# Seven products of halves instead of eight for 46 more weight chunks of a three-block transformer kernel

## The chip, the cores and the metric

One core of a Trainium2 chip runs the whole program. The metric is the device time of one execution in microseconds (us). PE is TensorE, DVE is VectorE, ACT is ScalarE, POOL is GpSimd, SP is SyncE, whose queue issues the weight transfers.

## What is computed

The reference takes 512 tokens of width 1024 through two layers of a first block and one of a second, all in 32-bit floats. What matters here are its large products of tokens and weights:

```python
# first block, twice
proj = x @ w_in[l]                       # 1024 x 8192: q, k, v, conv (3 x 512), memory query, gates (3 x 1024)
merged = (g[:, :, 0] * (y_attn @ w_br_attn[l]) + g[:, :, 1] * (y_conv @ w_br_conv[l])
          + g[:, :, 2] * (y_mem @ w_br_mem[l]))
mix = merged @ w_out[l]                  # then layer norm, 16 routed experts, layer norm
# second block, once
proj = h @ w_in                          # recurrent branch, state-space (S5) branch, gates (2 x 1024)
mixed = (g_rwkv * o_rwkv + g_s5 * o_s5) @ w_out[l]
z = h @ w_up                             # then convolution, gelu(gate) * val, @ w_down
```

Queries and keys are then rotated by position, the attention's output is normalised by head, and the gates go through a sigmoid.

## The kernel before, in words

**Tiles and chunks.** Tokens lie transposed: a buffer (XT, B[0] to B[5]) holds 8 tiles of 128 features x 512 tokens. Weights come in chunks of 2 MB, 1024 rows by 512 columns, into a ring of four slots. A chunk gives four output tiles. `project` (L445 to L452) makes one tile: 8 contraction steps (4 for br_conv, br_mem, br_rwkv and br_s5) of a 128x128 weight block against 512 tokens, into one of eight PSUM banks. A 32-bit matmul is two instructions in the trace, so a tile of 8 steps shows 16 of them, at L451.

**The ring.** The order of the chunks is a list (`layer_chunks`, L123; `SECOND`, L148). `place_stream` (L171) deals them to the slots in turn. SP issues them in this order (`issue_weights`, L327), each when the last user of its slot has ended, and waits in order. Some entries of the list are "unfilled": they take a slot as work space and nothing is loaded.

**Stages.** The program is a row of stages; at each stage's end all engines meet. The stages that the change touches: `qkv` (L465: 6 chunks; queries and keys are copied by ACT, rotated by a matmul at L491 and turned by DVE), `conv_and_memory_inputs` (L748: 4 chunks, mean squares of the attention's heads, the convolution, then the memory's keys and values at L787 and L796), `merge` (L1002: 6 gate chunks, whose tiles alternate with tiles of the branch products; ACT makes the sigmoid, DVE multiplies, L1066 and L1069, and adds, L1071), `out_projection` (L1089: 2 chunks), `mixer` (L1678: 4 full chunks and a half one, then the recurrent and S5 parts), `second_merge` (L2371: 4 gate chunks), `second_out` (L2423: 2 chunks).

**The tables.** In the second layer's `merge`, DVE and ACT also build the sine and cosine tables of S5, hung on the tile counter i: from i = 5 on DVE makes the turns of step i - 5 (L963 to L983), ACT its sines from i = 6 on (L985), DVE the cosines from i = 7 on (L996), and POOL stores each step to memory (L1082). There are 16 steps and two buffers, so a sine waits for the store of the step two before.

**The seven products.** `ffn_up` (L2456) already does Strassen's scheme for its 11 chunks: tokens and weights are split in halves both ways, DVE makes four sums of the token quarters once (L2602 to L2607), POOL four sums of the weight quarters per chunk into an unfilled slot (L2563 to L2568), and PE does seven products of quarters, each as two tiles of 4 contraction steps and 256 columns (L2486), 56 matmuls in place of 64 half-size ones. Three of the seven share a bank pair: between them ACT copies the partial sum out (L2540, L2545, L2548) or DVE adds it (L2618), and PE's next product waits for that. The last quarter is copied at L2553.

## Time and profile before

| what | us |
|---|---|
| three runs | 4003.45, 4010.04, 4012.88 (median 4010.04) |
| the profiled execution | 4005.88 |
| its span | 4004.1 |
| PE busy | 3497.4, 87% |
| DVE, ACT, POOL busy | 1234.2, 682.0, 354.1 |
| mean granted clock of PE | 0.923 of full speed |

The profile is of one execution. Matmuls are pipelined, so their durations overlap: the distance of two starts is what a matmul costs. Below, "[7.74 <-DMA ...]" at a row's end is the idle time of the engine before it and what ended it; "x16" is the number of instructions in a merged row. A row of windows gives us, then busy us (and count) of PE, PEld (weight loads), DVE, ACT and POOL, the granted clock, the DMA share and GB/s.

### The profile page before, as it was taken

The page shows a single profiled execution, that of the slowest core. Times are in us where ns is not written, and L with a number is a line of the kernel's source. Part 1 is how long each engine was busy: PE and PEld are TensorE (multiplying, and loading weights), DVE is VectorE, ACT ScalarE, POOL GpSimd, SP SyncE. Part 2 cuts the span into 40 slices and gives each one's busy share as a digit, 9 for nine tenths or more (in the row PEclk, how much of TensorE's full clock was granted, in tenths as well). Part 3 has the DMA queues.
Part 4 walks back from the last instruction along what each step waited for, and adds up shares of the span by engine and source line. Part 5 has one row for each costly group of instructions (what it writes and reads, how often), then busy time and mean ns, then how long its engine had stood idle before and what let it go on. Part 6 is the DMA issues. An engine that isn't in the chain of part 4 may idle for free. (4 is left out here: it accounts for less than half of the span.)

```text
span 4004.1 us, 31617 instructions
## 1 busy us (share of the span) xinstructions
PE 3497.4 (87%) x12180; PEld 1876.8 (47%) x12180; DVE 1234.2 (31%) x2278; ACT 682.0 (17%) x1420; POOL 354.1 (9%) x318
## 2 busy tenths in 40 slices
PE   7979999959998499899998699946979989879987
PEld 3444544434444244454443444423457744368843
DVE  2163301120002323442541100024176611167602
ACT  0051200020102102413340100112122210011100
POOL 0010000000000000000000100010045300034300
PEclk9999999979998699899999799967979979989998
DMA  4131121218895311021222398861100122112220
GB/s 173 63 142 63 64 84 63 84 75 291 327 331 209 123 63 63 22 84 71 77 114 112 144 330 327 305 226 55 71 18 27 54 100 79 42 42 85 105 84 21
DMA packets 52361, 481.86 MB, mean 120 GB/s; under 512 B 5936, under 2 KB 6320, under 8 KB 28400
## 3 DMA queue, kind: packets, MB, share of 16 engines
q1 hardware_dynamic: 26784, 378.77, 25.8%
q0 software_dynamic: 23840, 87.04, 5.6%
q10 hardware_dynamic: 1584, 13.93, 0.9%
q8 instruction: 106, 1.74, 0.2%
q14 instruction: 47, 0.39, 0.0%
HBM read 507.76 MB, written 60.03 MB: 142 GB/s over the span
## 5 line engine op out<-in xcount | busy, mean ns | idle before, releaser
L451 PE MATMUL bank<-XT,ring 128*128 128x512 f32 x1792 | 795.8, 599 | 60.8 <-PEq L548 29.2
L451 PE MATMUL bank<-B,ring 128*128 128x512 f32 x1600 | 703.2, 597 | 26.2 <-PEq L1603 15.5
L451 PEld LDWEIGHTS bank<-XT,ring 128*128 128x128 f32 x1792 | 343.8, 192 | 495.3 <-issue 478.1
L451 PEld LDWEIGHTS bank<-B,ring 128*128 128x128 f32 x1600 | 306.3, 192 | 414.9 <-issue 414.9
L1449 PE MATMUL bank<-ring,B 128*128 128x512 f32 x1024 | 450.8, 598 | 11.5 <-issue 11.2
L1449 PEld LDWEIGHTS bank<-ring,B 128*128 128x128 f32 x1024 | 193.4, 191 | 250.3 <-issue 232.5
L2486 PE MATMUL bank<-B,ring 128*128 128x256 f32 x1232 | 268.0, 381 | 15.4 <-PEq L1603 15.4
L2486 PEld LDWEIGHTS bank<-B,ring 128*128 128x128 f32 x1232 | 235.3, 191 | 48.5 <-issue 16.2
L1467 PE MATMUL bank<-ring,B 128*128 128x512 f32 x512 | 225.1, 592 | 0.0
L1501 DVE TENSOR_TENSOR B<-B,bank 128x512 f32<-128x512 f32 x46 | 31.6, 688 | 577.2 <-PE bank L1449 527.1
L2643 PE MATMUL bank<-B,ring 128*128 128x512 f32 x352 | 153.6, 599 | 11.1 <-PEq L2472 11.1
L1467 PEld LDWEIGHTS bank<-ring,B 128*128 128x128 f32 x512 | 97.1, 190 | 121.5 <-issue 121.5
L1482 ACT ACTIVATE B<-bank 128x512 f32<-128x512 f32 x92 | 50.1, 595 | 536.7 <-PE bank L1421 460.2
L1512 DVE COPY B<-bank 128x512 f32<-128x512 f32 x92 | 62.3, 690 | 171.6 <-PE bank L1467 169.2
L2643 PEld LDWEIGHTS bank<-B,ring 128*128 128x128 f32 x352 | 67.7, 193 | 96.5 <-issue 96.5
L510 PE MATMUL bank<-ring,XT 128*128 128x512 f32 x256 | 110.5, 592 | 0.0
L1043 ACT ACTIVATE B<-bank 128x512 f32<-128x512 f32 x48 | 28.7, 597 | 442.8 <-PE bank L451 442.8
L658 DVE CUSTOM_DVE_ANT_0 bank<-bank,rt 128x128 f32<-128x128 f32 (+3 forms) x128 | 60.6, 516 | 124.0 <-PE bank L600 122.6
L708 ACT ACTIVATE B<-bank,vecs 128x256 f32<-128x256 f32 (+3 forms) x160 | 81.4, 512 | 66.3 <-DVE vecs L658 54.4
L1526 POOL DMA_DIRECT2D slots_y<-B x46 | 24.7, 536 | 759.2 <-DVE B L1512 759.2
L619 PE MATMUL bank<-B 128*128 128x128 f32 x448 | 83.5, 324 | 9.1 <-ACT B L723 8.1
L1594 PE MATMUL bank<-const,B 128*128 128x128 f32 x64 | 12.3, 381 | 90.6 <-DVE B L1580 90.6
(423 smaller groups left out, 3480.6 us busy)
## 6 DMA issues: line engine op xcount, KB each, us to landing
ring<-in_w_expert SPq DMA_DIRECT2D x138, 2048.0 KB
ring<-in_w_static SPq DMA_DIRECT2D x79, 2048.0 KB
B<-slots_x POOLq DMA_DIRECT2D x46, 512.0 KB, 8.8
slots_y<-B POOLq DMA_DIRECT2D x46, 512.0 KB, 8.1
slots_x<-B POOLq DMA_DIRECT2D x23, 512.0 KB, 16.6
ring<-s_tables SPq DMA_DIRECT2D x4, 2048.0 KB
s_tables<-tmp POOLq DMA_DIRECT2D x8, 512.0 KB, 2.9
s_tables<-B POOLq DMA_DIRECT2D x8, 512.0 KB, 2.9
```

The lines of the kernel that those rows point to most:

```text
L451: ins = pe.matmul(bank[:, :], w(k, col), rhs(k), start=k == 0, stop=k == kts - 1)
L510: ins = pe.matmul(bank[:, :], m.XT[:, k, t * P:(t + 1) * P], slot[:, k, :], start=k == 0, stop=k == KT - 1)
L619: ins = pe.matmul(bank[:, qb * P:(qb + 1) * P], values(h, kb), mixT[u % 2][:, kb * P:(kb + 1) * P], start=kb == 0, stop=kb == nk // P - 1)
L658: ins = dve.tensor_tensor_reduce(bank[:, 0:nk], bank[:, 0:nk], m.rt[:, 4 * P - nk:4 * P], -scale, 3.0e38, ALU.add, ALU.min, low)
L708: ins = act.activation(prob[i % 2][c][:, 0:nk], bank[:, 0:nk], ACT.Exp, bias=v[:, 12 + s + c:13 + s + c], scale=-1.0 if mask else scale, a ...
L1449: ins = pe.matmul(bank[:, :], xbT[n % 2][:, k, :], slot[:, k, :], start=k == 0, stop=k == KT - 1)
L1467: ins = pe.matmul(bank[:, :], hidT[o % 2][:, k, :], slot[:, k, cols], start=k == 0, stop=k == 3)
L1482: act.activation(xbT[n % 2][:, 4 * i:4 * i + 4, :], bank[:, :].rearrange("p (a b) -> p a b", a=4), ACT.Copy).then_inc(bk.free_sem(("xbT", ...
L1501: ins = dve.tensor_tensor(hid[n % 2], silu[n % 2], bank[:, :], ALU.mult)
L1512: dve.tensor_copy(y[o % 2][:, i, :], bank[:, :]).then_inc(bk.free_sem(("y", l, o, i)), 1)
L2486: ins = pe.matmul(out, left[:, k, i * P:(i + 1) * P], right[:, k, :], start=start and k == 0, stop=k == 3, skip_group_check=not start)
L2643: ins = pe.matmul(bank[:, :], slot(k % 4, c), hidden_tile(m, k), start=k == 0, stop=k == FF_T - 1)
```

## The change

The seven products become a class, `SevenProducts`, and 46 more chunks use it: "in" 0 to 15 of both layers, "out" of both layers, the second block's "in2" except its half chunk 4, and "out2". Each gets a slot of sums behind it in the ring, and br_mem and br_s5 move behind the gate chunk that comes before their use. The six banks 0 to 5 serve the products; rotations, mean squares and branch tiles alternate in banks 6 and 7. In the stages with branch products, the four tiles of a gate chunk are now made together, then the four branch tiles; ACT copies the parts first and makes the sigmoids in place. Rotations and mean squares come in bunches of four behind the next chunk's first product (`pause`). POOL makes the weight sums, except in the second layer's `merge`, where it does so for the first chunk alone and DVE makes the others behind each chunk's last addition. In `out_projection` DVE does all copies. The buffers of the token sums are B[5] (or B[2], B[3], tmp), so the memset of B[5] moves from DVE in the first stage to POOL ahead of the stores in the first attention, and S5's scratch moves to `rt`. In `ffn_up` the convolution waits for each tile's own parts. The core of the diff:

```diff
+SPLIT = {"in", "out", "ffn_up", "out2"}
+EARLY_BRANCH = {("in", _l, 14): ("br_mem", _l, 0) for _l in range(DEPTH)}
+EARLY_BRANCH[("in2", 0, 7)] = ("br_s5", 0, 0)
...
+def with_sums(names):
+
+    out = []
+    for n in names:
+        out.append(n)
+        if n in EARLY_BRANCH:
+            out.append(EARLY_BRANCH[n])
+        if is_split(n):
+            out.append(sums_of(n))
+    return out
...
 def layer_chunks(l):
     names = [("in", l, j) for j in range(6)]
     names += [("in", l, j) for j in (6, 7, 8, 9)]
     names += [("mem_kv", l, 0), ("mem_kv", l, 1)]
     for b in range(3):
-        if b:
-            names.append((("br_conv", "br_mem")[b - 1], l, 0))
         for half in range(2):
             names.append(("in", l, 10 + 2 * b + half))
             if b == 0:
                 names.append(("br_attn", l, half))
+            elif (b, half) == (1, 0):
+                names.append(("br_conv", l, 0))
     names += [("out", l, 0), ("out", l, 1)]
-    return names
+    return with_sums(names)
...
+    def sum_tokens(self, dve):
+        made, x, T = self.m.tally("token_sums"), lambda k, n: quarter(self.x, k, n), self.T
+        dve.tensor_tensor(T[0], x(0, 1), x(0, 0), ALU.subtract).then_inc(made.up(), 1)
+        dve.wait_ge(*made.at(1))
+        dve.tensor_tensor(T[1], x(1, 1), T[0], ALU.subtract).then_inc(made.up(), 1)
+        dve.tensor_tensor(T[2], x(1, 1), x(0, 1), ALU.subtract).then_inc(made.up(), 1)
+        dve.wait_ge(*made.at(2))
+        dve.tensor_tensor(T[3], x(1, 0), T[1], ALU.subtract).then_inc(made.up(), 1)
+
+    def sum_weights(self, pool, n):
+        m, made, w, s = self.m, self.m.tally("weight_sums"), lambda p, k: self.w(n, p, k), lambda q: self.s(n, q)
+        pool.wait_ge(*m.landed(self.names[n]))
+        if m.earlier[m.index[sums_of(self.names[n])]] is not None:
+            pool.wait_ge(*m.slot_vacant(sums_of(self.names[n])))
+        pool.tensor_tensor(s(0), w(1, 0), w(1, 1), ALU.add).then_inc(made.up(), 1)
+        pool.wait_ge(*made.at(4 * n + 1))
+        pool.tensor_tensor(s(1), s(0), w(0, 0), ALU.subtract).then_inc(made.up(), 1)
+        pool.wait_ge(*made.at(4 * n + 2))
+        pool.tensor_tensor(s(3), w(0, 1), s(1), ALU.subtract).then_inc(made.up(), 1)
+        pool.tensor_tensor(s(2), w(0, 0), w(1, 0), ALU.subtract).then_inc(made.up(), 1)
+
+    def multiply(self, pe, n, tokens_left=False, pause=None):
+        m, bk, T, x = self.m, self.bk, self.T, lambda k, h: quarter(self.x, k, h)
+        name = self.names[n]
+        weights, tokens = m.tally("weight_sums"), m.tally("token_sums")
+
+        def product(kind, w, t, i, start):
+            out, part = self.out(kind, n, i), slice(i * P, (i + 1) * P)
+            for k in range(4):
+                left, right = (t[:, k, part], w[:, k, :]) if tokens_left else (w[:, k, part], t[:, k, :])
+                ins = pe.matmul(out, left, right, start=start and k == 0, stop=k == 3, skip_group_check=not start)
+            return ins
+
+        pe.wait_ge(*m.landed(name))
+        for i in range(2):
+            pe.wait_ge(*bk.vacant(self.key("x", n, i)))
+            product("x", self.w(n, 0, 0), x(0, 0), i, True).then_inc(m.tally("p1").up(), 1)
+        if pause:
+            pause()
+        pe.wait_ge(*tokens.at(1))
+        pe.wait_ge(*weights.at(4 * n + 1))
+        for i in range(2):
+            pe.wait_ge(*bk.vacant(self.key("z", n, i)))
+            product("z", self.s(n, 0), T[0], i, True).then_inc(m.tally("p5").up(), 1)
+        pe.wait_ge(*tokens.at(2))
+        pe.wait_ge(*weights.at(4 * n + 2))
+        for i in range(2):
+            pe.wait_ge(*m.tally("p1_kept").at(2 * n + i + 1))
+            product("x", self.s(n, 1), T[1], i, False).then_inc(m.tally("p6").up(), 1)
+        pe.wait_ge(*weights.at(4 * n + 3))
+        for i in range(2):
+            pe.wait_ge(*m.tally("p5_kept").at(2 * n + i + 1))
+            product("z", self.s(n, 3), x(1, 1), i, False).then_inc(bk.full_sem(self.key("z", n, i)), 1)
+        pe.wait_ge(*tokens.at(3))
+        pe.wait_ge(*weights.at(4 * n + 4))
+        for i in range(2):
+            pe.wait_ge(*m.tally("p6_kept").at(2 * n + i + 1))
+            product("x", self.s(n, 2), T[2], i, False).then_inc(m.tally("p7").up(), 1)
+        m.last_uses[m.index[sums_of(name)]] = m.tally("p7").last()
+        for i in range(2):
+            pe.wait_ge(*bk.vacant(self.key("w", n, i)))
+            product("w", self.w(n, 0, 1), x(1, 0), i, True).then_inc(bk.full_sem(self.key("w", n, i)), 1)
+        pe.wait_ge(*tokens.at(4))
+        for i in range(2):
+            pe.wait_ge(*m.tally("corner").at(2 * n + i + 1))
+            product("x", self.w(n, 1, 1), T[3], i, False).then_inc(bk.full_sem(self.key("x", n, i)), 1)
+        m.last_use(name, self.key("x", n, 1))
...
+    def add_sums(self, dve, n, dest):
+        m, bk = self.m, self.bk
+        for i in range(2):
+            dve.wait_ge(*m.tally("p6_kept").at(2 * n + i + 1))
+            dve.wait_ge(*bk.made(self.key("z", n, i)))
+            dve.tensor_tensor(dest(0, 1, i), self.out("z", n, i), dest(0, 1, i), ALU.add).then_inc(bk.free_sem(self.key("z", n, i)), 1)
+        for i in range(2):
+            dve.wait_ge(*m.tally("p5_kept").at(2 * n + i + 1))
+            dve.wait_ge(*m.tally("p7").at(2 * n + i + 1))
+            dve.tensor_tensor(dest(1, 1, i), self.out("x", n, i), dest(1, 1, i), ALU.add).then_inc(m.tally("corner").up(), 1)
+        for i in range(2):
+            dve.wait_ge(*bk.made(self.key("w", n, i)))
+            dve.tensor_tensor(dest(0, 0, i), self.out("w", n, i), dest(0, 0, i), ALU.add).then_inc(bk.free_sem(self.key("w", n, i)), 1)
...
 def qkv(m, l):
...
+                for c in range(4):
+                    seven.finished(pe, n, c // 2, c % 2)
+                    pe.wait_ge(*bk.vacant(("rot", l, n, c)))
+                    bank = bk.bank(("rot", l, n, c))
+                    pe.matmul(bank[:, :], m.c("rotate"), raw[n // 2][:, 4 * (n % 2) + c, :], start=True, stop=True).then_inc(bk.full_sem(("rot", l, n, c)), 1)
+
+            for n in range(6):
+                seven.multiply(pe, n, tokens_left=n >= 4, pause=(lambda: rotate(n - 1)) if 0 < n < 5 else None)
...
 def merge(m, l):
...
+            for n in range(6):
+                seven.multiply(pe, n)
+                for b, j in jobs[4 * n:4 * n + 4]:
+                    if b == 0:
+                        w = ("br_attn", l, j // 4)
+                        pe.wait_ge(*m.landed(w))
+                        project(m, pe, ("branch", l, b, j), by512(m.slot_of(w)), j % 4, KT, rhs[0])
+                        if j % 4 == 3:
+                            m.last_use(w, ("branch", l, b, j))
+                    else:
+                        w = (("br_conv", "br_mem")[b - 1], l, 0)
+                        pe.wait_ge(*m.landed(w))
+                        project(m, pe, ("branch", l, b, j), by1024(m.slot_of(w)), j, CT, rhs[b])
+                        if j == KT - 1:
+                            m.last_use(w, ("branch", l, b, j))
 
         @block.scalar
         def _(act):
-            for i, (b, j) in enumerate(jobs):
-                act.wait_ge(*bk.made(("gate", l, b, j)))
-                bank = bk.bank(("gate", l, b, j))
-                if i >= 4:
-                    act.wait_ge(*bk.read_done(("branch", l, *jobs[i - 4])))
-                act.activation(sig[:, i % 4, :], bank[:, :], ACT.Sigmoid).then_inc(bk.free_sem(("gate", l, b, j)), 1)
-                if tables and i == 1:
-                    tables.steps(act)
-                if tables and i == 3:
-                    tables.first_angles(act)
-                if tables and 6 <= i < 22:
-                    tables.sines(act, i - 6)
+            for n in range(6):
+                if n:
+                    act.wait_ge(*bk.read_done(("branch", l, *jobs[4 * n - 1])))
+                for part in (seven.keep_first, seven.keep_fifth, seven.keep_sixth, seven.last_quarter):
+                    part(act, n, copy_to(place))
+                for c in (2, 3, 0, 1):
+                    seven.finished(act, n, c // 2, c % 2)
+                    act.activation(sig[:, c, :], sig[:, c, :], ACT.Sigmoid).then_inc(m.tally("gates").up(), 1)
+                for i in range(4 * n, 4 * n + 4):
+                    if tables and i == 1:
+                        tables.steps(act)
+                    if tables and i == 3:
+                        tables.first_angles(act)
+                    if tables and 6 <= i < 22:
+                        tables.sines(act, i - 6)
...
+            seven.sum_tokens(dve)
+            for n in range(6):
+                seven.add_sums(dve, n, place)
+                if tables and n < 5:
+                    seven.sum_weights(dve, n + 1)
+                for c in range(4):
+                    i, (b, j) = 4 * n + c, jobs[4 * n + c]
+                    if c == 0:
+                        dve.wait_ge(*m.tally("gates").at(4 * n + 4))
+                    dve.wait_ge(*bk.made(("branch", l, b, j)))
+                    bank = bk.bank(("branch", l, b, j))
+                    if b == 0:
+                        dve.tensor_tensor(merged[:, j, :], bank[:, :], sig[:, c, :], ALU.mult).then_inc(bk.free_sem(("branch", l, b, j)), 1)
+                    else:
+                        t = sig[:, 4 + c, :]
+                        dve.tensor_tensor(t, bank[:, :], sig[:, c, :], ALU.mult).then_inc(bk.free_sem(("branch", l, b, j)), 1)
+                        dve.wait_ge(*bk.read_done(("branch", l, b, j)))
+                        dve.tensor_tensor(merged[:, j, :], merged[:, j, :], t, ALU.add).then_inc(m.tally("dve_step").up(), 1)
+                        dve.wait_ge(*m.tally("dve_step").last())
+                    if tables and i == 2:
+                        tables.angles(dve)
+                    if tables and i == 4:
+                        tables.constants(dve)
+                    if tables and 5 <= i < 21:
+                        tables.turns(dve, i - 5)
+                    if tables and 7 <= i < 23:
+                        tables.cosines(dve, i - 7)
+
+        @block.gpsimd
+        def _(pool):
+            if tables is None:
+                for n in range(6):
+                    seven.sum_weights(pool, n)
+                return
+            for dst, src in ((tables.t_row, m.dram["rows"][:, 1, :]), (tables.cfull, m.dram["s5_c"])):
+                pool.dma_start(dst, src).then_inc(m.table_rows, 16)
+            seven.sum_weights(pool, 0)
...
 def out_projection(m, l):
...
+            seven.sum_tokens(dve)
+            for n in range(2):
+                for part in (seven.keep_first, seven.keep_fifth, seven.keep_sixth):
+                    part(dve, n, with_input(n))
+                seven.add_sums(dve, n, place(n))
+                seven.last_quarter(dve, n, with_input(n))
```

`keep_first`, `keep_fifth`, `keep_sixth` and `last_quarter` copy one part each, for i = 0 and 1, when PE has made it, and raise the counts `p1_kept`, `p5_kept`, `p6_kept` and the bank's free count. `finished` waits until both parts of a tile have been read.

## Rows read from the trace of the kernel before

**Rows 1.** The page: busy time of each engine over the whole span.
```profile
PE 3497.4 (87%) x12180; PEld 1876.8 (47%) x12180; DVE 1234.2 (31%) x2278; ACT 682.0 (17%) x1420; POOL 354.1 (9%) x318
```

**Rows 2.** The page's groups by line: busy us, mean ns, idle before.
```profile
L451 PE MATMUL bank<-XT,ring 128*128 128x512 f32 x1792 | 795.8, 599 | 60.8 <-PEq L548 29.2
...
L2486 PE MATMUL bank<-B,ring 128*128 128x256 f32 x1232 | 268.0, 381 | 15.4 <-PEq L1603 15.4
L2486 PEld LDWEIGHTS bank<-B,ring 128*128 128x128 f32 x1232 | 235.3, 191 | 48.5 <-issue 16.2
```

**Rows 3.** PE's timeline, first layer's qkv and gates: start us, us, instructions.
```profile
68.20 1.02 PE L491 MATMUL bank<-B,const 128*128 128x512 f32 x2
69.06 7.03 PE L451 MATMUL bank<-XT,ring 128*128 128x512 f32 x16
...
584.58 7.03 PE L451 MATMUL bank<-XT,ring 128*128 128x512 f32 x16
591.45 3.60 PE L451 MATMUL bank<-B,ring 128*128 128x512 f32 x8
594.88 7.03 PE L451 MATMUL bank<-XT,ring 128*128 128x512 f32 x16
```

**Rows 4.** Windows: the feed-forward's stage, us and busy time by engine.
```profile
3538.40:3806.70 268.30, 267.99 (x1232) 235.33 (x1232) 181.90 (x210) 45.27 (x109) 116.89 (x44) 0.99 0.24 87
```

**Rows 5.** PE's timeline, gate stages of both layers.
```profile
663.54 3.60 PE L451 MATMUL bank<-B,ring 128*128 128x512 f32 x8
674.88 8.87 PE L451 MATMUL bank<-XT,ring 128*128 128x512 f32 x16 [7.74 <-DMA ring<-in_w_static]
...
2034.23 10.14 PE L451 MATMUL bank<-XT,ring 128*128 128x512 f32 x16 [7.74 <-DMA ring<-in_w_static]
```

**Rows 6.** DVE's and PE's timeline at the feed-forward's end.
```profile
3807.16 0.55 DVE L2577 TENSOR_SCALAR B<-B,par 128x512 f32<-128x512 f32 x1 [3.71 <-ACT B L2553]
...
3816.12 0.69 DVE L2586 TENSOR_TENSOR B<-B 128x512 f32<-128x512 f32 x1
...
3817.51 12.80 PE L2643 MATMUL bank<-B,ring 128*128 128x512 f32 x24 [11.07 <-PEq L2472]
```

**Rows 7.** DVE's and POOL's timeline at the feed-forward's start.
```profile
3538.30 1.23 DVE L2602 TENSOR_TENSOR B<-B 128x1024 f32<-128x1024 f32 x1 [0.52 <-PEq L1603]
3539.56 3.25 DVE L2604 TENSOR_TENSOR B<-B 128x1024 f32<-128x1024 f32 x1
...
3538.35 3.38 POOL L2563 TENSOR_TENSOR ring<-ring 128x1024 f32<-128x1024 f32 x1 [344.03 <-POOLq L1603]
...
3551.57 2.34 POOL L2563 TENSOR_TENSOR ring<-ring 128x1024 f32<-128x1024 f32 x1
```

**Rows 8.** PE's timeline where out_projection follows the gates.
```profile
761.67 3.67 PE L451 MATMUL bank<-B,ring 128*128 128x512 f32 x8 [2.39 <-PEq L1010]
```

**Rows 9.** DVE's and ACT's timeline, one table step of the second layer's gates.
```profile
1954.49 0.49 DVE L969 TENSOR_SCALAR tmp<-rotary,s_columns 128x512 f32<-128x512 f32 x1 [4.73 <-issue]
...
1959.04 0.42 DVE L999 TENSOR_SCALAR B<-B 128x512 f32<-128x512 f32 x1
1960.09 0.69 DVE L1071 TENSOR_TENSOR B<-B 128x512 f32<-128x512 f32 x1
...
1962.74 1.28 ACT L991 ACT_TABLE_LOAD   x1 [0.84 <-DMA s_tables<-B]
1964.03 0.63 ACT L991 ACTIVATE B<-B 128x512 f32<-128x512 f32 x1
```

**Rows 10.** Groups by line: reciprocals and memory projection of both layers.
```profile
L834 DVE RECIPROCAL B<-B 128x512 f32<-128x512 f32 x16 | 53.6, 3353 | 16.9 <-ACT B L812 16.4
...
L787 PE MATMUL bank<-memT,ring 128*128 128x256 f32 x128 | 28.0, 379 | 0.0
...
L796 PE MATMUL bank<-ring,memT 128*128 128x512 f32 x64 | 27.8, 592 | 0.0
```

**Rows 11.** ACT's timeline, a copy of a product in the feed-forward.
```profile
3563.01 0.38 ACT L2553 ACTIVATE B<-bank 128x256 f32<-128x256 f32 x1 [11.70 <-PE bank L2486]
```

More of the change, by code:

```diff
@@ L160, in static_names @@
         out += layer_chunks(l)
[L161 removed]
+    return [n for n in out + SECOND if n not in S5_STREAM and not unfilled(n)]
 def stream_names():
@@ L465, in qkv, with copy_to, within @@
+def copy_to(dest):
+    return lambda act, p, h, i, src: act.activation(dest(p, h, i), src, ACT.Copy)
+def within(tile):
+    return lambda p, h, i: tile(2 * p + i)[:, HALF * h:HALF * h + HALF]
 def qkv(m, l):
@@ L779, in _ @@
                     pe.matmul(bank[:, :], m.c("ones"), sq[:, j, :], start=True, stop=True).then_inc(bk.full_sem(("rms", l, j)), 1)
+            for n in range(4):
+                seven.multiply(pe, n, pause=(lambda: mean_squares(n - 1)) if n in (1, 2) else None)
             pe.wait_ge(m.memory_loaded, 2 * 16)
@@ L839, in _ @@
+            for n in range(4):
+                if n in (1, 2):
+                    variances(n - 1)
+                if n == 3:
+                    scaled(range(4))
+                seven.add_sums(dve, n, place(n))
+            for n in (1, 2):
+                for i in range(2):
+                    seven.finished(dve, n, 0, i)
+                    seven.finished(dve, n, 1, i)
+            seven.finished(dve, 0, 1, 1)
             for j in range(CT):
@@ L851, in _ @@
                 dve.wait_ge(*m.tally("dve_step").last())
+                scaled(range(4 + j, 5 + j))
+        @block.gpsimd
+        def _(pool):
+            for n in range(4):
+                seven.sum_weights(pool, n)
         m.issue_weights(block)
@@ L1009, in merge @@
     tables = S5Tables(m) if l == DEPTH - 1 else None
+    seven = SevenProducts(m, m.XT, blocks(m.B[5][:, 0:4, :], m.B[5][:, 4:8, :]))
+    place = within(lambda c: sig[:, c, :])
     with m.stage() as block:
-        for b, j in jobs:
-            bk.plan(("gate", l, b, j))
-            bk.plan(("branch", l, b, j))
+        for n in range(6):
+            seven.chunk(("in", l, 10 + n))
+            for b, j in jobs[4 * n:4 * n + 4]:
+                bk.plan(("branch", l, b, j), 6 + j % 2)
         @block.tensor
@@ L1086, in merge, with with_input @@
         m.issue_weights(block)
 def out_projection(m, l):
-    bk = m.banks
+    seven = SevenProducts(m, m.B[0], blocks(m.B[2][:, 0:4, :], m.B[2][:, 4:8, :]))
+    place = lambda n: within(lambda c: m.B[1][:, 4 * n + c, :])
+    skipped = lambda n: within(lambda c: m.XT[:, 4 * n + c, :])
+    def with_input(n):
+        return lambda dve, p, h, i, src: dve.scalar_tensor_tensor(place(n)(p, h, i), skipped(n)(p, h, i), ALPHA, src, ALU.mult, ALU.add)
     with m.stage() as block:
-        for j in range(KT):
-            bk.plan(("mix", l, j))
+        for n in range(2):
+            seven.chunk(("out", l, n))
@@ L2141, in _ @@
         def _(pool):
+            for n in range(4):
+                seven.sum_weights(pool, n)
             for j in range(CT):
@@ L2377, in second_merge @@
     jobs = [(b, j) for b in range(2) for j in range(KT)]
+    seven = SevenProducts(m, m.B[0], blocks(m.B[3][:, 0:4, :], m.B[3][:, 4:8, :]))
+    place = within(lambda c: sig[:, c, :])
     with m.stage() as block:
-        for b, j in jobs:
-            bk.plan(("gate2", b, j))
-            bk.plan(("branch2", b, j))
+        for n in range(4):
+            seven.chunk(("in2", 0, 5 + n))
+            for b, j in jobs[4 * n:4 * n + 4]:
+                bk.plan(("branch2", b, j), 6 + j % 2)
         @block.tensor
@@ L2481, in _ @@
+    seven = SevenProducts(m, m.B[0], blocks(m.B[1][:, 0:4, :], m.B[1][:, 4:8, :]))
+    place = lambda j: within(lambda c: z_tiles[4 * (j % 2) + c])
+    with m.stage() as block:
+        for j in range(n_chunks):
+            seven.chunk(("ffn_up", 0, j))
         @block.tensor
         def _(pe):
-            def product(out, left, right, i, start):
-                for k in range(4):
-                    ins = pe.matmul(out, left[:, k, i * P:(i + 1) * P], right[:, k, :], start=start and k == 0, stop=k == 3,
-                                    skip_group_check=not start)
-                return ins
@@ L2529, in gelu @@
+            for j in range(n_chunks):
+                seven.multiply(pe, j)
         def gelu(act, j, i):
```

617 lines of the change are left out of this document (276 added, 341 removed).

## The prediction

> **What bounds the kernel now.** I read the page first: TensorE (PE) is busy for 87% of the span [rows 1], and no other engine comes near that share. Then the groups by line: the plain projection helper (L451) and the seven-product form that the feed-forward already has (L2486) stand side by side in one trace [rows 2]. Then PE's order of time in the stages that the change touches: one 512-wide tile of eight contractions follows another every 591.45 - 584.58 = 6.87 us, a four-contraction tile takes 3.43 us, and the projection stages have hardly an idle microsecond in them [rows 3]. So these stages end when PE ends, and what counts is PE's work per chunk and any new wait of PE.
>
> **The product itself.** A chunk is four tiles: 4 x 6.87 = 27.5 us [rows 3]. In the feed-forward the same chunk is done as 7 x 2 x 4 products of width 256, each in two passes, 112 instructions. [...] Vector (DVE), Scalar (ACT) and GpSimd (POOL) did the sums and copies beside it at no cost. I take 24.2. The gain is 3.3 us a chunk, not an eighth (3.4), times 46 chunks: **-151 us**. [...]
>
> [...]
>
> **Other gains.** The ring's order changes: br_mem now comes behind the fifth gate chunk, whose load no longer waits for the slot of br_conv. Before, PE waited 7.74 us there in each layer, and ran its next 16 matmuls in 8.87 and 10.14 us instead of 7.03 after it [rows 5]: 2 x 7.74 + 1.84 + 3.11 = **-20 us**. At the feed-forward's end the convolution waits tile by tile, not for all six banks. Before, DVE started at 3807.2 and ended at 3816.8, then ffn_down began [rows 6]. Now the first of its four convolutions (about 2 us each: 9.65 us hold four and two short products) can start about 3 us before PE's end: **-4 us** (0 to -6).
>
> **Ring slots.** Every split chunk takes a second slot for its sums, so only one chunk is loaded ahead. A load starts when its slot's last user ends and lands 7.8 us later (667.1 to 674.9) [rows 5], inside a 24 us chunk; POOL's four sums follow in 4 x 2.34 to 3.38 us [rows 7], so they are ready 17 to 21 us into the chunk before. That hides. Not hidden: the first output chunk of both layers and of the second block now takes the slot of the last branch matrix (br_mem, br_s5), which PE uses to the very end of the stage. The load lands 7.8 us behind PE's end; the stage change itself took 2.4 us [rows 8]. So 5.4 us more, and some 2 us of lower clock after it [rows 5]: 3 x 7.4 = **+22 us** (12 to 30).
>
> **Stage starts.** DVE's four token sums and POOL's first four weight sums run together and stretch each other from 1.23 to 3.25 us and from 2.34 to 3.38 us [rows 7]. In the feed-forward PE didn't wait for them, since its first two products take 6.9 us. The other stages have the same order: 0. In out_projection DVE also does every copy, behind 11 us of token sums if these are stretched; but there the weights land late, POOL waits, and DVE's sums take 5 us before PE begins: 0 (to +5 each if that cover fails). The memset of B[5] moves to POOL ahead of 23 stores in attention, beside 90 us of other work: 0.
>
> **Rotations.** Four rotations now come in one bunch behind the first product, with two banks. The fourth waits until DVE has read the second: DVE needs two passes of 0.69 us [rows 9] per tile against 0.86 us of PE [rows 3]. About 0.7 us x 8 chunks = **+6 us** (0 to 12). The mean squares in the convolution stage bunch the same way, 4 x 0.4 = **+2 us**. That stage's tail: after PE's last gate-side product DVE has 4 convolutions (3.6 us) and 4 reciprocals with a multiply (3.35 + 0.7) [rows 10], 30.7 us started 3 us early, so it ends 27.7 us behind PE's last product. The memory projection covers it: 14.0 + 13.9 us [rows 10]. 0 (to +3).
>
> **The second layer's gates.** Here DVE is asked for more. It also makes the S5 tables: one step is 4.97 us (1954.49 to 1959.46) and a merge 1.4 us [rows 9], and the change gives it the weight sums as well. Before, that fitted: 6.4 us a tile against 10.3. Now follow a chunk of the second or third branch, T = 0 at the end of its products. DVE makes the next chunk's sums until 5.1 us (4 x 1.26), then four rounds of merge and table step of 6.4 us each; it reads the last branch tile at 25.0 and the third round's cosine ends at 24.3. ACT's fourth sine waits for the store of that cosine, which took 3.3 us (1959.46 to 1962.74) [rows 9], and takes 1.9 us: 29.5. Only then does ACT, in order, keep the next chunk's first product, 0.38 us [rows 11]: 29.9. PE has finished four branch tiles at 13.7 and two products at 20.6 and then needs that copy. It waits 9.3 us, and about 2 us go on a lower clock. This happens behind the chunks n = 2, 3 and 4 (the first branch's tiles are twice as long and cover it): 3 x 11.3 = **+34 us**. Lower bound: if only the last read counted, 25.4 - 20.6 = 4.8 us each; upper: 12 us and 3 us of clock each: 14 to 45. At the stage's end the last table steps and stores run until about 20 us, 7 us behind PE, as long as the load of the output chunk that is counted above.
>
> **Mixer.** The shifts end 3.3 us instead of 2 us behind the projections, but DVE then waits for ACT anyway; S5's first table lands 8 us behind and is first read 13 us behind: 0 (to +4).
>
> **Sum.** -151 - 20 - 4 + 22 + 6 + 2 + 34 = -111 us. The profiled execution took 4005.9 us (span 4004.1), 4 us below the median of the three runs, 4010.0. So 3895 against the profiled one, and 3896 with a little of that difference: **3896 us**. Small changes under 0.2%, 8 us, can't be told from none here.
>
> **Rivals.**
> A. *The gates of the second layer don't stall* (ACT gets its table work done in time). Then the 34 us stay away: 3862. For it: DVE has some 25 us of work for 38 us of PE if one takes the sums alone; against: ACT is in order and its last sine stands behind DVE's last but one step. 0.13.
> B. *DVE and POOL block each other in more places than at stage starts.* The stretched passes of rows 7 would come back in rotations, shifts and merges, where each copy or sum that PE waits for would be 1 to 2 us later: 20 to 30 chunks by 1.5 us, +30 to +45, 3926 to 3941. Against: eleven feed-forward chunks had this mixture with no idle PE [rows 4]. [...] 0.22.
> C. *Slower: sums arrive too late.* With one chunk of look-ahead, landing (7.8) and four sums (9.4 to 13.5) must fit in 24.2 us. There are 3 us left in the worst case. If a sum took 4.8 us instead of 3.4, every back-to-back chunk would wait: 7.8 + 19.2 - 24.2 = 2.8 us. It decides against the change from 2.4 us on each of the 46 (111 / 46); at 2.8 us: 4024 us. Against: 3.38 us is what a fully busy DVE makes of one sum, and 2.34 us stands beside an idle DVE [rows 7]. 0.02.
> D. [...] The rows deny it: 0.01.
> My forecast has the rest, 0.62.
>
> **How the numbers follow.** The forecast's own terms leave 3875 to 3925. A's end is inside if the range goes to 3858, and B's lower half if it goes to 3936. **3858 to 3936.** Forecast, A and B are faster by far more than 8 us (0.97, of which I give 0.01 to an end within 8 us, where B and the beginnings of C would meet): faster 0.96, within 0.01, slower 0.03 (C and D).
>
> **What would show it.** In the trace after: PE passes of width 256 every 0.216 us, 24.2 us a chunk; no 7.7 us wait inside either gate stage; a wait for DMA of 5 to 8 us at the head of out_projection (twice) and second_out; in the second layer's gate stage three waits of PE for ACT of about 9 us in the sixth-product group, none in the first layer's. Rotations with gaps under 1 us. Wrong would be: waits of PE for POOL or for the weight DMA in the middle of stages (C), two-input DVE passes of 1.5 us with PE waiting for them (B), or no ACT waits in the gates (A).

## The result and the profile after

The changed kernel takes 3912.1 us (median of 4 runs, 3908.4 to 3920.5) against 4008.0 (4 runs, 4003.5 to 4012.9) of the kernel before beside it: a ratio of 0.9763, with an interval from 0.9743 to 0.9784. The forecast was 3896 in a range from 3858 to 3936. So the sign and the size were right, and the point was 16 us too low. The profiled execution took 3909.9 us (span 3907.9).

First the page's busy times, to be laid beside [rows 1].

```profile
PE 3362.8 (86%) x14388; PEld 2304.8 (59%) x14388; DVE 1483.9 (38%) x2625; ACT 714.2 (18%) x1631; POOL 770.3 (20%) x483
```

PE lost 135 us of busy time, the span only 96. The rest is in PE's waits. Next its timeline at the end of the first layer's values, where the attention follows: start, us, instructions. Values are made in the tokens-left form, in which the block of tokens is the one that PE loads and the weights stream past it.

```profile
182.48 3.62 PE L573 MATMUL bank<-ring,B 128*128 128x256 f32 x16
185.93 3.62 PE L573 MATMUL bank<-ring,XT 128*128 128x256 f32 x16
189.38 3.62 PE L573 MATMUL bank<-ring,B 128*128 128x256 f32 x16
193.89 0.93 PE L793 MATMUL bank<-B 64*128 64x128 f32 x8 [0.89 <-PEq L677]
```

32 passes start in 189.38 - 182.48 = 6.90 us, one every 0.2156 us, so a chunk of 112 takes 24.15 us where it took 27.5 [rows 3]. Then the list of PE's waits: what it waited for, us in total, times, longest. Of some 40 kinds these belong to the change.

```profile
PE bank L573 <- ACT B L657: 25.3, 3, 11.6
PE bank L573 <- DMA ring<-in_w_static: 16.9, 2, 8.9
PE bank L573 <- PEq L1228: 15.1, 1, 15.1
PE bank L482 <- DVE B L1287: 6.1, 4, 1.8
PE bank L695 <- DVE tmp L722: 2.8, 8, 0.4
PE bank L573 <- DVE B L1327: 1.5, 1, 1.5
```

Three waits for ACT's copies, two for a load, one at the end of a stage, four for DVE's merges, eight in the rotations, one for a copy of DVE's in the second layer's output projection; none for POOL, and the 7.74 us waits of [rows 5] are gone. I then took each stage's length from PE's first instruction in it to its first in the next, in both traces. "Foreseen" is what the prediction's terms give for that stage; a wait at the head of a stage counts with the stage ahead of it.

| stage | before | after | change | foreseen |
|---|---|---|---|---|
| queries, keys, values, layer 1 | 181.7 | 165.5 | -16.2 | -17 |
| the same, layer 2 | 181.8 | 165.0 | -16.8 | -17 |
| convolution, layer 1 and 2 | 292.5 | 267.1 | -25.4 | -24 |
| gates, layer 1 | 287.0 | 264.0 | -23.0 | -24 |
| **gates, layer 2** | 288.2 | 310.7 | **+22.6** | **+9** |
| output, layer 1 and 2 | 114.1 | 105.8 | -8.4 | -9 |
| mixer, the whole stage | 492.2 | 478.1 | -14.1 | -13 |
| second block's gates | 167.3 | 159.9 | -7.4 | -8 |
| second block's output | 58.6 | 52.0 | -6.5 | -5 |
| feed-forward | 279.1 | 275.3 | -3.8 | -4 |
| all the rest | | | +3 | 0 |

Only one row is off by more than 4 us, and it holds nearly all of the miss. Here is that stage in PE's timeline.

```profile
1875.51 10.46 PE L482 MATMUL bank<-B,ring 128*128 128x512 f32 x24
1887.73 3.67 PE L482 MATMUL bank<-B,ring 128*128 128x512 f32 x8 [1.76 <-DVE B L1287]
...
1905.16 6.17 PE L573 MATMUL bank<-B,ring 128*128 128x256 f32 x16 [6.85 <-ACT B L657]
...
1937.21 3.67 PE L482 MATMUL bank<-B,ring 128*128 128x512 f32 x8 [1.77 <-DVE B L1287]
1959.42 6.34 PE L573 MATMUL bank<-B,ring 128*128 128x256 f32 x16 [11.63 <-ACT B L657]
1991.64 3.67 PE L482 MATMUL bank<-B,ring 128*128 128x512 f32 x8 [1.77 <-DVE B L1287]
2009.07 5.42 PE L573 MATMUL bank<-B,ring 128*128 128x256 f32 x16 [6.85 <-ACT B L657]
2039.42 3.67 PE L482 MATMUL bank<-B,ring 128*128 128x512 f32 x8 [0.82 <-DVE B L1287]
2058.22 9.89 PE L573 MATMUL bank<-B,ring 128*128 128x256 f32 x32 [15.12 <-PEq L1228]
2069.60 41.68 PE L573 MATMUL bank<-B,ring 128*128 128x256 f32 x192 [1.50 <-DVE B L1327]
```

The three waits for ACT are there (25.3 us), and after each the next 16 passes take 5.42 to 6.34 us instead of 3.62: 7.1 us in all. Beside them stand two things that were not foreseen: a wait for DVE at the fourth branch tile in four of the six chunks (6.1 us in all), and 15.12 us at the stage's end, where I had 7.8.

The windows of the trace show the clock around the first wait: from and to, length, busy time of PE, PEld, DVE, ACT and POOL, then the granted clock, DMA share and GB/s.

```profile
1891.20:1898.30 7.10, 7.10 (x33) 5.89 (x31) 6.72 (x14) 3.01 (x6) 0.53 (x1) 1.00 0.18 74
1905.20:1911.10 5.90, 5.90 (x16) 4.81 (x17) 0.76 (x2) 1.02 (x4) 0.53 (x1) 0.58 0.22 89
1911.20:1921.00 9.80, 9.80 (x47) 8.64 (x46) 2.13 (x5) 0.38 (x1) 0.00 (x0) 1.00 0.01 2
```

Before the wait of 6.85 us the granted clock was 1.00 of full speed, behind it 0.58, and 6 us later 1.00 again. Last, who holds ACT: its timeline around the second wait. L1207 is a sine of the tables, L657 the copy that PE waits for; it comes behind the sines.

```profile
1954.99 0.63 ACT L1207 ACTIVATE tmp<-tmp 128x512 f32<-128x512 f32 x1 [13.42 <-DMA s_tables<-tmp]
1957.19 0.63 ACT L1207 ACTIVATE B<-B 128x512 f32<-128x512 f32 x1 [0.39 <-DMA s_tables<-B]
...
1958.91 1.19 ACT L657 ACTIVATE B<-bank 128x256 f32<-128x256 f32 x4
```

The store that the first of these waits for is this one in POOL's timeline:

```profile
1943.09 0.53 POOL L1313 DMA_DIRECT2D s_tables<-tmp  x1 [5.80 <-DVE tmp L1215]
```

Issued at 1943.1, it let the sine go at 1955.0: 11.9 us. SP had issued two weight loads of 2 MB just before, the first at 1940.9. The page's median of these stores is 2.9 to 3.1 us. That is what made this wait 11.6 us where the other two are 6.9.

### The profile page after: what moved, and what is told of

Read it like the earlier page. It is cut to its first block and busy times, and to the rows that moved or that the text cites. A ratio compares the mean times of both kernels' runs of the same rounds, so it can differ in the third digit from the quotient of the medians.

```text
span 3907.9 us, 37207 instructions
## 1 busy us (share of the span) xinstructions
PE 3362.8 (86%) x14388; PEld 2304.8 (59%) x14388; DVE 1483.9 (38%) x2625; ACT 714.2 (18%) x1631; POOL 770.3 (20%) x483
## 5 line engine op out<-in xcount | busy, mean ns | idle before, releaser
L573 PE MATMUL bank<-B,ring 128*128 128x256 f32 x4336 | 966.6, 384 | 92.0 <-PEq L1843 30.9
L573 PEld LDWEIGHTS bank<-B,ring 128*128 128x128 f32 x4336 | 834.6, 193 | 220.9 <-issue 84.9
L557 POOL TENSOR_TENSOR ring<-ring 128x1024 f32<-128x1024 f32 x52 | 132.1, 2540 | 1285.4 <-DMA ring<-in_w_static 438.1
L573 PE MATMUL bank<-XT,ring 128*128 128x256 f32 x1344 | 308.1, 383 | 44.5 <-PEq L741 28.4
L657 ACT ACTIVATE B<-bank 128x256 f32<-128x256 f32 x356 | 135.1, 383 | 1133.9 <-PE bank L573 1133.7
L482 PE MATMUL bank<-B,ring 128*128 128x512 f32 x704 | 308.0, 596 | 8.1 <-DVE B L1287 6.1
L573 PEld LDWEIGHTS bank<-XT,ring 128*128 128x128 f32 x1344 | 257.6, 192 | 85.8 <-issue 50.8
L482 PEld LDWEIGHTS bank<-B,ring 128*128 128x128 f32 x704 | 134.1, 191 | 171.5 <-issue 170.6
L636 DVE TENSOR_TENSOR B<-bank,B 128x256 f32<-128x256 f32 x96 | 40.6, 424 | 317.4 <-PE bank L573 316.7
L2831 PE MATMUL bank<-B,ring 128*128 128x512 f32 x352 | 153.8, 600 | 7.3 <-PEq L2743 7.3
L1722 ACT ACTIVATE B<-bank 128x512 f32<-128x512 f32 x92 | 50.1, 595 | 543.2 <-PE bank L1661 461.4
L561 POOL TENSOR_TENSOR ring<-ring 128x1024 f32<-128x1024 f32 x52 | 136.1, 2617 | 4.1
L559 POOL TENSOR_TENSOR ring<-ring 128x1024 f32<-128x1024 f32 x52 | 134.1, 2579 | 4.1
L562 POOL TENSOR_TENSOR ring<-ring 128x1024 f32<-128x1024 f32 x52 | 132.0, 2539 | 0.0
L2831 PEld LDWEIGHTS bank<-B,ring 128*128 128x128 f32 x352 | 67.7, 193 | 92.9 <-issue 92.9
```

The source lines that it names most:

```text
L482: ins = pe.matmul(bank[:, :], w(k, col), rhs(k), start=k == 0, stop=k == kts - 1)
L557: pool.tensor_tensor(s(0), w(1, 0), w(1, 1), ALU.add).then_inc(made.up(), 1)
L559: pool.tensor_tensor(s(1), s(0), w(0, 0), ALU.subtract).then_inc(made.up(), 1)
L561: pool.tensor_tensor(s(3), w(0, 1), s(1), ALU.subtract).then_inc(made.up(), 1)
L562: pool.tensor_tensor(s(2), w(0, 0), w(1, 0), ALU.subtract).then_inc(made.up(), 1)
L573: ins = pe.matmul(out, left, right, start=start and k == 0, stop=k == 3, skip_group_check=not start)
```

## The experiments

My theory after this reading: (1) the passes give what was summed; (2) in the second layer's gates ACT's copies stand behind four table steps in a row, which DVE's work paces; (3) the heads (the first products) of the output projections wait for a load whose slot comes free last. Each kernel below is the changed kernel with one edit, or several where it says so, and is compared with its 3912.1 us; the ratio is always to the kernel before. Comments in the diffs are explanations, not code. One warning for every comparison of profiled spans: stages that no edit touches differ between executions. The first layer's attention, from its first matmul to the next stage's, took 88.7 us in the changed kernel's profile and 90.2 to 96.8 in those of the seven runs. So the effect of an edit is read from the stage that it edits.

**1. The second layer's gate chunks whole again.**

```diff
 def is_split(name):
+    if name[0] == "in" and name[1] == DEPTH - 1 and name[2] >= 10:
+        return False
...
 def merge(m, l):
+    if l == DEPTH - 1:
+        return merge_whole(m, l)      # the loop of before, with its ring order
```

> The second layer's six gate chunks are made whole again, with the old loop and the old ring order there; the other 40 chunks stay split. My theory: that stage loses about 22 us by the split (310.7 after against 288.2 before), so it comes back to about 288, the wait of 15.1 us at the head of the second output projection falls to 2 to 9, and the whole is 20 to 30 us faster than the changed kernel: 3882 to 3892 against 3912. Rival (every chunk gains its 3.28 us here too, the waits are somewhere else or would be there anyway): about 20 us slower, 3930.

Measured: 3894.6 us (3889.8 to 3897.0), ratio 0.9715 (0.9698 to 0.9732). Undoing a part of the change makes the kernel 17.5 us faster, so the split of these six chunks costs more than it gives; I had said 20 to 30. The stage took 286.8 us (before 288.2, changed 310.7), 23.9 less. The profiled spans differ by only 12.8: 1.8 went back in the output projection behind it (56.1 instead of 54.3), the rest lies in stages that the edit doesn't touch, 4.5 of it in the first layer's attention. PE's timeline shows the stage and the projection: the old wait for a load is back, and a wait for DVE's copies appears once the load no longer covers them.

```profile
1951.97 8.86 PE L486 MATMUL bank<-XT,ring 128*128 128x512 f32 x16 [7.69 <-DMA ring<-in_w_static]
2038.59 7.14 PE L577 MATMUL bank<-B,ring 128*128 128x256 f32 x32 [2.23 <-PEq L1230]
2050.01 43.37 PE L577 MATMUL bank<-B,ring 128*128 128x256 f32 x192 [4.27 <-DVE B L1422]
```

**2. POOL makes the weight sums there, not DVE.**

```diff
-                if tables and n < 5:
-                    seven.sum_weights(dve, n + 1)
...
+            for n in range(3):
+                seven.sum_weights(pool, n)
             pool.wait_ge(*m.tally("s5_matrix").at(1))
...
             for s in range(16):
+                if s in (1, 5, 9):
+                    seven.sum_weights(pool, 3 + s // 4)
                 pool.wait_ge(*m.tally("s5_cosines").at(s + 1))
```

> In the second layer's gate stage POOL makes the weight sums instead of DVE (4 x 1.23 = 4.9 us for each of five chunks), between its stores. In the changed kernel DVE's table work of a chunk (4 x 6.33 us) begins only behind its sums, and each sine follows DVE by 3.6 us. Theory 1, DVE's amount sets it: the waits of 6.9, 11.6 and 6.9 us at the sixth product lose 4.9 us each and the three waits of 1.8 us for the bank go, 15 to 20 us faster, 3892 to 3897. Theory 2, DVE and POOL slow each other when both have two inputs (1.23 to 3.25 and 2.34 to 3.38 us at the start of the feed-forward): DVE's multiplies stretch over the 13.5 us in which POOL sums, the table work is not earlier, and the waits stay or grow: 3905 to 3925. Theory 3, only ACT's order counts and DVE is not the clock of the sines: no change within 3 us.

Measured: 3929.5 us (3922.5 to 3929.9), ratio 0.9801 (0.9783 to 0.9819), 17 us slower. That is theory 2, and above its range of 3905 to 3925; but the stage itself took 321.6 us instead of 310.7, 10.8 more, and the rest is in stages that the edit doesn't touch. The waits for ACT fell little (25.3 to 22.0 us), those for DVE's merges grew from 6.1 to 15.7. DVE's timeline behind the third chunk, whose products ended at 1880.6, and POOL's sums beside it:

```profile
1884.75 0.69 DVE L1285 TENSOR_TENSOR B<-bank,B 128x512 f32<-128x512 f32 x1 [6.94 <-ACT B L1261]
1885.47 0.81 DVE L1287 TENSOR_TENSOR B<-B 128x512 f32<-128x512 f32 x1
1886.32 2.47 DVE L1185 TENSOR_SCALAR tmp<-rotary,s_columns 128x512 f32<-128x512 f32 x1
1888.82 2.45 DVE L1187 TENSOR_SCALAR tmp<-tmp 128x512 f32<-128x512 f32 x1
...
1885.81 2.69 POOL L561 TENSOR_TENSOR ring<-ring 128x1024 f32<-128x1024 f32 x1
1888.46 2.53 POOL L562 TENSOR_TENSOR ring<-ring 128x1024 f32<-128x1024 f32 x1
```

The changed kernel's DVE at the same place:

```profile
1880.57 0.68 DVE L1287 TENSOR_TENSOR B<-bank,B 128x512 f32<-128x512 f32 x1
```

Two readings. DVE begins its merges 4.1 us behind the products, where with its sums it began 5.1 us behind (1880.57 against 1875.51): the sums had stood almost wholly in the time that DVE waits for the sigmoids anyway, so taking 4.9 us away gave 1. And while POOL sums, two passes with a *single* tensor input, 0.49 and 0.43 us otherwise, take 2.47 and 2.45, about as long as one of POOL's (2.35 to 2.7): 4.0 us more, so that each chunk's table work ends 3 us later in spite of the earlier start. So what the prediction's rival B describes appears where POOL sums beside table steps; giving the sums to DVE was right.

**3. The ring's order.** The first output chunk gets the slot of the sixth gate chunk. The slot of the last branch matrix, which is free last, goes to the second output chunk. Told as the order of the list, not as code:

```text
-    ..., in14, br_mem, sums14, in15, sums15, out0, sums_out0, ...
+    ..., in14, in15, sums14, br_mem, sums15, out0, sums_out0, ...
```

(The second block likewise.) 

> Ring order alone: the first output chunk gets the slot of a gate chunk that is free two chunks earlier, and the late slot goes to a sums slot. Theory (the wait at the head of the output projections is the load that waited for the last branch tile): the waits of 8.9 and 8.1 us at the heads of the first and third output projection fall to 0 to 3 us, and with the load gone that competes with the last table stores the 15.1 us at the second one falls to 8 or less: 15 to 25 us faster in all, less up to 5 us for each projection whose token sums are no longer covered by the load: 3892 to 3907. Rival (the wait is DVE's token sums, and the load is hidden behind them): no change, 3912.

Measured: 3901.5 us (3897.1 to 3902.7), ratio 0.9734 (0.9717 to 0.9750), 10.6 us faster in the medians, though the two intervals still overlap; the span of the profiled runs fell by 8.5. The three gate stages and the projections behind them take 12.2 less together. So the theory holds, inside its 3892 to 3907, and its rival, no change, is out. The waits of 8.90 and 8.05 us at two heads became 2.20 and 2.21, but DVE's copies then hold PE a little later. One part failed: at the second layer the wait at the stage's end fell only from 15.1 to 12.2, where I had 8 or less. PE's timeline:

```profile
709.75 8.83 PE L583 MATMUL bank<-B,ring 128*128 128x256 f32 x32 [2.20 <-PEq L1238]
721.16 4.14 PE L583 MATMUL bank<-B,ring 128*128 128x256 f32 x11 [2.58 <-DVE B L1337]
...
2057.03 9.74 PE L583 MATMUL bank<-B,ring 128*128 128x256 f32 x32 [12.20 <-PEq L1238]
```

There the last store (issued at 2046.3) had again a weight load beside it, issued at 2044.9: the second output chunk's. It was one load where the changed kernel has two, and the store took 8.4 us instead of 11.3.

**4. The table steps spread over the chunk.** The same instructions; two of a chunk's four tables are made while its products run.

```diff
                 for part in (seven.keep_first, seven.keep_fifth, seven.keep_sixth):
                     part(act, n, copy_to(place))
+                if n >= 2:
+                    sines((4 * n - 6, 4 * n - 5))
                 seven.last_quarter(act, n, copy_to(place))
...
+                if 1 <= n <= 4:
+                    sines((4 * n - 4, 4 * n - 3))
...
-                seven.add_sums(dve, n, place)
+                seven.add_lower(dve, n, place)     # then a cosine and a turn, n >= 2
+                seven.add_corner(dve, n, place)    # then a cosine and a turn, n >= 2
+                seven.add_upper(dve, n, place)
...
+                if tables and 1 <= n <= 4:         # behind the merges
+                    for k in range(2):
+                        tables.cosines(dve, 4 * n - 4 + k)
+                        turns(4 * n - 2 + k)
```

> The same work in the second layer's gate stage in another order: two of the four tables of a chunk are made while its seven products run, between ACT's copies and DVE's adds, and two behind them. Theory (the copies wait because they stand behind four tables in a row): the waits of 6.9, 11.6 and 6.9 us for ACT go, with their 7 us of lowered clock and part of the 15.1 us at the stage's end: 30 to 40 us faster, 3872 to 3882. Rival (DVE and ACT have too much work for the shorter chunk wherever it stands: 25.3 us of tables, 4.9 of sums, 2.5 of adds and 0 to 3 of merges beside 51 us of PE a chunk): the waits move to the corner adds and to the seventh product, gain under 10 us.

Measured: 3868.3 us (3864.1 to 3871.0), ratio 0.9651 (0.9634 to 0.9668): 43.8 us faster than the changed kernel, more than the 30 to 40 I had said, because the bank waits went too. The stage takes 268.5 us instead of 310.7. In PE's timeline of it the branch tiles run in one piece, one wait of 2.00 is left inside, and the end is the load's.

```profile
1918.54 14.06 PE L482 MATMUL bank<-B,ring 128*128 128x512 f32 x32
1955.31 5.38 PE L573 MATMUL bank<-B,ring 128*128 128x256 f32 x16 [2.00 <-DVE B L643]
1960.53 13.90 PE L482 MATMUL bank<-B,ring 128*128 128x512 f32 x32
1998.43 13.90 PE L482 MATMUL bank<-B,ring 128*128 128x512 f32 x32
2020.99 14.24 PE L573 MATMUL bank<-B,ring 128*128 128x256 f32 x57 [8.65 <-DMA ring<-in_w_static]
```

It was the order, not the amount: nothing was taken from any engine. The bank waits went with it, since DVE now reads four merges without a table step between them. The gain adds up: ACT waits 25.3, clock 7.1, bank waits 6.1, the end 15.1 - 8.65 = 6.5, less 2.0 and 1.8 (16 passes in 5.38 instead of 3.62) for the wait that is left = 41.2 of the stage's 42.2. The last store lands at 1995.8 here, long before the stage's end, so that end waits for the load alone.

**5. The edits of 3 and 4 together.**

> The tables spread over the chunk (3868.3 alone) and the new ring order (10.4 us faster alone) together. If the two are independent: 3856 to 3860. Theory: more, since with both the last table store no longer ends beside the load of the first output chunk, so that the three waits of 8.0 to 8.8 us that remain at the heads of the output projections all go to 2 to 4: 3848 to 3856. Rival (the heads are held by DVE and POOL as soon as the load is early): 3860 to 3868.

Measured: 3857.0 us (3843.8 to 3863.5), ratio 0.9622 (0.9593 to 0.9652). That is what independence gives; the "more" did not come. All three heads are at 2.2 us now, but two waits for DVE's first copies (2.58 and 4.27 us) took their place. That is the rival's mechanism, though the time stays under its 3860 to 3868. The timeline is the second layer's.

```profile
2009.90 7.14 PE L583 MATMUL bank<-B,ring 128*128 128x256 f32 x32 [2.20 <-PEq L1248]
2021.32 44.00 PE L583 MATMUL bank<-B,ring 128*128 128x256 f32 x192 [4.27 <-DVE B L1372]
```

**6. Queries, keys and values whole again** (edit 1's form, for the twelve chunks of both layers, with the loops of before).

```diff
 def is_split(name):
+    if name[0] == "in" and name[2] < 6:
+        return False
```

> Queries, keys and values of both layers are computed whole again, 12 of the 46 chunks, with the old loops; the rest as changed. Theory (a split chunk saves 3.28 us of TensorE, and its rotations cost it some 6 us less per stage than a stall would): the two stages go from 165.5 and 165.0 us back to about 182 each, and the whole is 31 to 39 us slower: 3943 to 3951. Rival (the gain comes from the ring and from the stalls that went, not from the passes): under 10 us slower, 3912 to 3922.

Measured: 3945.1 us (3939.1 to 3953.3), ratio 0.9853 (0.9831 to 0.9875): 33.0 us slower, as the theory said, 2.75 us a chunk with rotations, start and values counted in. The first layer's attention begins at 211.75 and PE's first product at 29.24, a stage of 182.5 us; split it was 193.89 - 28.39 = 165.5. The second layer's stage went from 165.0 to 181.5.

```profile
29.24 11.20 PE L484 MATMUL bank<-XT,ring 128*128 128x512 f32 x19 [29.24 <-PEq L750]
...
211.75 0.93 PE L802 MATMUL bank<-B 64*128 64x128 f32 x8 [0.94 <-PEq L673]
```

**7. As 5, with DVE's first copies between the token sums** in both output projections.

```diff
+    def sum_tokens(self, dve, after_second=None, after_third=None):
...
         dve.tensor_tensor(T[1], x(1, 1), T[0], ALU.subtract).then_inc(made.up(), 1)
+        if after_second:
+            after_second()             # keep_first of chunk 0
         dve.tensor_tensor(T[2], x(1, 1), x(0, 1), ALU.subtract).then_inc(made.up(), 1)
+        if after_third:
+            after_third()              # keep_fifth of chunk 0
```

> As the run with both edits (3857.0), and in both first-block output projections DVE makes its first four copies out of the banks between the token sums and no longer behind all four of them. Theory (with the load early, the 4.3 us wait at the sixth product is DVE's order: four sums of 1.2 to 3.4 us ahead of the first copy): the waits of 4.3 and 2.6 us go with 1 to 2 us of clock each, 5 to 11 us faster, 3846 to 3852. Rival (the copies themselves are stretched by POOL's sums as much as they move ahead): within 3 us, 3854 to 3860.

Measured: 3846.0 us (3840.7 to 3853.0), ratio 0.9598 (0.9580 to 0.9616), 11.1 us faster than 5. The intervals of the two overlap, but the two stages show it: the first layer's projection takes 49.9 us instead of 56.1, and the second's, which took 2066.59 - 2009.90 = 56.7 us in 5, takes 2056.74 - 2005.19 = 51.6, together 11.3 less. It is the best version: 66 us under the changed kernel, 163 under the one before. In the second layer PE runs through both chunks:

```profile
2005.19 50.27 PE L587 MATMUL bank<-B,ring 128*128 128x256 f32 x224 [2.20 <-PEq L1252]
2056.74 7.10 PE L1417 MATMUL bank<-B,const 128*128 128x512 f32 x16 [1.28 <-PEq L1378]
```

## Why the prediction held, and where it missed

**The product term (-151)** held. A chunk takes 24.15 us where I took 24.2, in the tokens-left form shown above and in the weights-left one (192 passes in 41.68 us, at 2069.60), and run 6 gives the right share back when twelve chunks are undone. No run shows 24.2 itself: it was my estimate from [rows 4], where 1232 passes in 268.0 us are one every 0.2175, 24.4 us a chunk, less the first one's start; what the changed kernel shows is 24.15. That more weight loads must be hidden (14388 instead of 12180 instructions) cost nothing, so rival D, in which each load would take its time beside its matmul, is out: the page's 256-wide group has a load of 0.193 us for each pass and they follow every 0.216. In the kernel before, its loads of 0.191 us lay under those every 0.2175 us in the same way [rows 2, 4].

**Ring order and feed-forward (-20, -4)** held: no wait of 7.7 us is left in the gates, and the feed-forward is 3.8 us shorter.

**The late load of the first output chunk (+22)** held in place and nearly in size: 8.90 and 8.05 us of wait in two of three stages against 7.8 foreseen. Run 3 took it away, which shows the cause. In the third stage, the second layer's, it was covered by something longer (below).

**Rotations (+6)** held. The list of waits has eight idle stretches of 0.35 us, 2.8 in all, but what a bunch costs is read from the starts:

```profile
58.29 3.00 PE L695 MATMUL bank<-B,const 128*128 128x512 f32 x6
61.64 1.10 PE L695 MATMUL bank<-B,const 128*128 128x512 f32 x2 [0.36 <-DVE tmp L722]
62.58 7.07 PE L573 MATMUL bank<-B,ring 128*128 128x256 f32 x32
```

62.58 - 58.29 = 4.29 us, where four rotations without a wait take 4 x 0.86 = 3.44 [rows 3]. That is 0.85 for each bunch, where I had 0.7, and 6.8 in all. The +2 for the mean squares did not come: PE waits nowhere for them.

**The second layer's ACT waits (+34)** held: 25.3 us of waiting and 7.1 of lower clock, 32.4. Place, number (three) and cause are as written, and run 4 shows the cause by removing them. The size of each is off both ways: 6.85, 11.63, 6.85 for 9.3. ACT's copy came 29.1 us behind the products (1904.65 against 1875.51), as good as my 29.9; but PE needed it 1.8 us later than I had, since it had waited for the bank. And one of the three had a store of 11.9 us in it where I had 3.3.

**What failed**, two terms of the same stage:
- "At the stage's end the last table steps and stores run until about 20 us, 7 us behind PE, as long as the load." PE ended at 2043.1 and went on at 2058.2, 15.1 us later. ACT's last sine had waited for a store, so the last cosine came at 2043.9 and its store was issued at 2044.6. Priced with a store that had the queues to itself, it would have landed near 2048; beside two weight loads issued at 2043.2 it landed near 2056 (2.2 us for the change of stage taken off). I had two transfers end at the same time and took the longer, where the store took 11.3 us beside the loads for 2.9 without. It costs 7.3 us. Runs 3 and 4 bear it out: with one load in place of two the store takes 8.4 us, and with the store out of the way the end is the load's 8.65. The trace of the kernel before had already shown it. Its line for the stores into `s_tables` is

```profile
DMA to landing us min/median/max: 2.9/2.9/10.6
```

and the longest of them, issued at 2032.0, stood behind three weight loads issued from 2026.5 on. I had taken one row of 3.3 us for all.

- I had priced the pair of banks for the rotations only. The branch tiles alternate between two banks as well, and in this stage DVE puts a table step between two merges: the fourth tile waits for the read of the second, 1.8 us in three chunks and 0.8 in a fourth: 6.1 us. The prediction had even written the rounds of 6.4 us down, and had used them only for the last read.

7.3 and 6.1, less the 1.6 by which the ACT term was too high, make 11.8 of the 13.7 us by which the stage missed its +9. With them the sum is -99 against -96 measured in the profiled runs; the last 3 are spread over stages that the change doesn't touch.

**Rivals.** A (no stall, 3862) is out as a forecast, but it is what run 4 makes of the kernel: 3868. B was not seen in the changed kernel: every long wait of PE has another cause. The nearest is the 1.50 us in the second layer's output projection, where DVE's copies stand behind token sums that POOL's sums stretch (3.25 us for 1.23); I had given that place 0 to 5. Run 2 shows it in the table steps (2.47 and 2.45 us for 0.49 and 0.43). C is out: PE never waited for POOL. Runs 5 and 7 lie under the range's end, because they also take away the late load and mend the order of the copies, which I had counted as fixed.

## What to carry to other kernels

When one engine's work shrinks, go through the order of instructions on each engine beside it and ask what stands *ahead* of the small copy that the fast engine waits for; here the same instructions in another order were worth 44 us, almost half of what the change itself brought. Price a stage's end with the transfers that run beside each other there, not with the median of one alone; the trace before the change may already hold such a row. When a wait goes, look at what it had covered: behind the late load stood DVE's token sums, behind DVE's weight sums the wait for the sigmoids.

## What the runs showed of the hardware

- A 0.5 MB store took 2.9 us in the changed kernel's median. With weight loads of 2 MB issued up to 2.2 us before it, it took 8.4 to 9.2 us behind one load (runs 3, 4, 5 and 7) and 10.4 to 13.1 behind two (the changed kernel and runs 2 to 7). In the changed kernel the first packet of such a store moved 4.0 us after its issue, that of an undisturbed one after 1.1.
- While POOL added with two inputs, two of DVE's passes with one tensor input took 2.47 and 2.45 us for 0.49 and 0.43 (run 2). I had reckoned with two-input passes only, as in [rows 7]. DVE's two passes ended 0.3 us behind the POOL passes of 2.69 and 2.53 us beside them. In the changed kernel, where DVE makes these weight sums, none of the 16 passes of each of the two kinds took more than 0.57 and 0.43 us.
- After waits of 6.85 and 11.63 us the granted clock was 0.58 and 0.57 for about 6 us, and 16 passes took 6.2 and 6.3 us for 3.6; after another of 6.85 it was 0.68, and they took 5.4. So the price did not follow the length of the wait. After waits of 2.20 us it went both ways: 32 passes took 7.14 us in run 5's second layer (clock 1.00) and 8.83 in run 3's first (0.81). After 4.27 us, 192 passes took 43.37 us in run 1 and 44.00 in run 5, elsewhere 41.68.
